# Seven smaller products for one more outer product of a feed-forward, and the order of the last loads

## The reference, cut to what matters

```python
D_FF = ((8 * D_MODEL // 3 + 255) // 256) * 256      # 2816 = 22 tiles of 128

def swiglu(h, w_gate, w_up, w_down):
    return (jax.nn.silu(h @ w_gate) * (h @ w_up)) @ w_down
```

## Time and profile before

| what | value |
|---|---|
| median of three runs | 5031.72 us (5031.61 to 5036.39) |
| the profiled execution | 5037.27 us, span 5035.5 us |
| TensorE matmul busy | 4921.3 us, 98% |
| VectorE busy | 3003.9 us, 60% |
| ScalarE busy | 865.2 us, 17% |
| feed-forward loop, block 1 to 10 | from 1384.24 us to about 1823.7 us |
| product with w_down | from 1829.79 us |

### The profile page before, as it was taken

The page is one execution under the profiler, slowest core; times in us unless marked ns, Lnnn a source line. Parts: engine busy times, 40 slices in busy tenths (PEclk is TensorE's granted clock), DMA queues, the critical chain, the costliest instruction groups (busy, mean ns, idle before and its releaser), DMA issues. The chain is left out here.

```text
span 5035.5 us, 68191 instructions
## 1 busy us (share of the span) xinstructions
PE 4921.3 (98%) x26175; PEld 3429.4 (68%) x26175; DVE 3003.9 (60%) x5245; ACT 865.2 (17%) x1673; POOL 72.0 (1%) x96
## 2 busy tenths in 40 slices
PE   8999999999999999999999799999999999999998
PEld 4545556855477754447666695959788696969695
DVE  3434445645388863553666575757667575767686
ACT  3611211133211100160444100000000000000010
POOL 0000000000000000000000000000000000000110
PEclk9999999999999999999999799999999999999999
DMA  5145032411222263433221354544445454545575
GB/s 209 40 148 182 26 105 96 152 59 62 61 67 71 72 204 100 159 109 117 106 90 57 114 185 147 194 164 160 167 158 189 150 181 177 185 172 201 180 284 217
DMA packets 396603, 694.44 MB, mean 138 GB/s; under 512 B 19896, under 2 KB 171003, under 8 KB 394234
## 3 DMA queue, kind: packets, MB, share of 16 engines
q1 hardware_dynamic: 382072, 641.80, 36.9%
q0 software_dynamic: 9920, 36.19, 2.0%
q10 hardware_dynamic: 4290, 12.11, 0.6%
HBM read 575.21 MB, written 114.83 MB: 137 GB/s over the span
## 5 line engine op out<-in xcount | busy, mean ns | idle before, releaser
L4880 PE MATMUL psum<-arena 128*128 128x128 f32 (+2 forms) x10752 | 1235.7, 276 | 2.9 <-issue 2.7
L4880 PEld LDWEIGHTS psum<-arena 128*128 128x128 f32 x10752 | 1225.7, 191 | 6.8 <-issue 6.8
L4859 PE MATMUL psum<-arena 128*128 128x512 f32 x1568 | 689.6, 595 | 2.8 <-DVE arena L4472 2.4
L4589 DVE TENSOR_TENSOR arena<-arena 128x1024 f32<-128x1024 f32 x448 | 539.4, 1224 | 64.5 <-issue 39.6
L4859 PEld LDWEIGHTS psum<-arena 128*128 128x128 f32 x1568 | 292.1, 190 | 363.3 <-issue 355.4
L1559 PE MATMUL psum<-arena 128*128 128x256 f32 x1400 | 305.4, 379 | 0.0
L1559 PEld LDWEIGHTS psum<-arena 128*128 128x128 f32 x1400 | 266.0, 190 | 44.7 <-issue 9.6
L1630 PE MATMUL psum<-arena 128*128 128x512 f32 x616 | 267.4, 596 | 5.9 <-DMA arena<-in_ffn_w_down 5.9
L4764 ACT ACTIVATE arena<-psum 128x288 f32<-128x288 f32 (+1 forms) x112 | 44.6, 398 | 1151.0 <-PE psum L4880 1072.6
L2219 PE MATMUL psum<-arena 128*128 128x256 f32 (+1 forms) x968 | 239.6, 407 | 1.4 <-PEq L112 1.4
L4467 DVE TENSOR_TENSOR arena<-arena 128x512 f32<-128x512 f32 x112 | 77.6, 693 | 252.5 <-PE psum L4865 157.7
(11 more groups left out here) (636 smaller groups left out, 6167.4 us busy)
## 6 DMA issues: line engine op xcount, KB each, us to landing
arena<-in_moe_w_gate SPq DMA_DIRECT2D x112, 1024.0 KB
arena<-in_moe_w_up SPq DMA_DIRECT2D x112, 1024.0 KB, 7.3
arena<-in_moe_w_down SPq DMA_DIRECT2D x112, 1024.0 KB, 6.7
y_dram<-zeros SPq DMA_DIRECT2D x1, 23040.0 KB
x_dram<-arena SPq DMA_DIRECT2D x32, 512.0 KB, 4.0
arena<-in_ab_w_in SPq DMA_DIRECT2D x7, 2048.0 KB, 8.9
arena<-z_dram SPq DMA_DIRECT2D x8, 1664.0 KB, 7.4
arena<-in_c_w_in SPq DMA_DIRECT2D x6, 2048.0 KB, 11.8
```

The source lines that it names most:

```text
L4589: V.tensor_tensor(to, left, right, ALU.subtract).then_inc(t_up, 1)
L4859: return nc.tensor.matmul(g.ps[:, bank, :], left, right, start=(i == 0), stop=(i == STEPS - 1))
L4880: last = nc.tensor.matmul(g.ps[:, bank, f * HT:f * HT + N // 2], right[:, k, f * P:(f + 1) * P], left[:, k, 0:N // 2], start=(k == 0), sto ...
```

## The change

Outer product 4 is made of seven smaller ones as well. So `SPLIT` gets a 4, a fourth set of inner token sums lies at column 33024 (until then free during the loop), and the VectorE order of a block changes: `inner_weights(n, 4)` comes ahead of `combine(n, 2)`, the difference t4 moves from between the combines of 2 and 3 to ahead of `combine(n, 4)`, and `combine(n, 4)` takes the place of the plain addition that made `part`. On ScalarE `take_corner(n, 4)` takes the place of `take_whole(n, 4)`. In SP's order of the loop, the load of raw quarter (1,1) is ahead of the store of Q22. At the end of the loop `bring_low(3)` is after product 4 instead of ahead of product 3, and the last piece of `low` is loaded in two halves, one after the last reader of raw quarter (1,0) and one after product 6, both ahead of the store of Q22. There are no new functions.

```diff
-    SPLIT = (2, 3, 5, 6, 7)
+    SPLIT = (2, 3, 4, 5, 6, 7)
@@ SP, loop
-                store(n, Q22, 1, 1)
                 sp.wait_ge(pm, groups_done(n, 6))
                 load(n + 1, 1, 1)
+                store(n, Q22, 1, 1)
@@ SP, after the loop
-            bring_low(3)
             sp.wait_ge(pm, groups_done(N, 3))
             bring_low(0)
             bring_low(1)
@@
             for t in (2, 3):
                 fetch_x(t, x_low)
+            bring_low(3)
             sp.wait_ge(pm, groups_done(N, 5))
             bring_low(2)
             load_low(1, 1, 2, b11)
+            sp.wait_ge(outer_made, 4 * N)
+            sp.dma_start(low[0][:, 0:2, :], quarter(1, 1)[:, 0:2, :]).then_inc(b11, 16)
+            sp.wait_ge(pm, groups_done(N, 6))
+            sp.dma_start(low[0][:, 2:4, :], quarter(1, 1)[:, 2:4, :]).then_inc(b11, 16)
             store(N, Q22, 1, 1)
-            sp.wait_ge(pm, groups_done(N, 6))
-            load_low(1, 1, 0, b11)
@@ TensorE
-                    whole_product(b, 4)
+                    pe.wait_ge(x_summed, 3)
+                    split_product(it, b, 4)
@@ ScalarE
                 take_corner(n, 3)
-                act.wait_ge(st_e, 16 * n)
-                take_whole(n, 4, e5)
+                take_corner(n, 4)
@@ VectorE, block_of_features
                 outer(n, t3, raw[1, 1], raw[0, 1])
+                inner_weights(n, 4)
                 dve.wait_ge(st_a, 16 * (2 * n - 1))
-                dve.wait_ge(whole, 2 * n + 1)
+                dve.wait_ge(whole, n + 1)
                 combine(n, 2, za, e1)
-                outer(n, t4, raw[1, 0], t2)
                 dve.wait_ge(st_b, 16 * n)
                 combine(n, 3, zb, e1, u)
                 gate(n, Q11)
                 inner_weights(n, 5)
-                dve.wait_ge(whole, 2 * n + 2)
-                V.tensor_tensor(part, u, e5, ALU.add).then_inc(joined, 1)
+                outer(n, t4, raw[1, 0], t2)
+                combine(n, 4, zb, u, part)
                 inner_weights(n, 6)
                 za_is_free(n)
                 combine(n, 5, za, u, u)
-                dve.drain()
-                V.tensor_tensor(e5, u, e5, ALU.add).then_inc(joined, 1)
+                dve.wait_ge(st_e, 16 * n)
+                dve.drain()
+                V.tensor_tensor(e5, u, zb[:, 0:4, :], ALU.add).then_inc(joined, 1)
@@ VectorE, ahead of the loop
-            for q in (2, 3, 6):
+            for q in (2, 3, 4, 6):
                 inner_tokens(q)
                 in_place(q).then_inc(x_summed, 1)
```

More of the change, by code:

```diff
@@ L1327, in ffn_stage @@
     RIGHTS = (raw[0, 0], raw[1, 0], t2, t1, t3, raw[1, 1], t4)
-    SPLIT = (2, 3, 5, 6, 7)
+    SPLIT = (2, 3, 4, 5, 6, 7)
     WAYS = len(SPLIT)
-    inner = [[A.at(o + 512 * q, 2, 256) for q in range(2)] + [A.at(last, 2, 256)] for o, last in ((24576, 25600), (26112, 27136), (30208, 31744), (35840, 36864), (37376, 38400))]
+    inner = [[A.at(o + 512 * q, 2, 256) for q in range(2)] + [A.at(last, 2, 256)] for o, last in ((24576, 25600), (26112, 27136), (33024, 34560), (30208, 31744), (35840, 36864), (37376, 38400))]
     ring = [[A.at(12288 + 1024 * r + 256 * q, 2, P) for q in range(4)] for r in range(2)]
@@ L1577, in _ @@
                     pe.wait_ge(hidden, 2)
-                    pe.wait_ge(combed, it * (2 * WAYS) + (WAYS * (c - 1) + 4))
+                    pe.wait_ge(combed, it * (2 * WAYS) + (WAYS * (c - 1) + 5))
                     whole_product(b, 1)
@@ L1583, in _ @@
                     pe.wait_ge(x_summed, 1)
-                    pe.wait_ge(combed, it * (2 * WAYS) + (WAYS * (c - 1) + 5))
+                    pe.wait_ge(combed, it * (2 * WAYS) + (WAYS * (c - 1) + 6))
                     split_product(it, b, 2)
@@ L1588, in _ @@
                     pe.wait_ge(outer_made, it * 8 + (4 * c - 2))
-                    pe.wait_ge(whole, it * 4 + (2 * c + 1))
+                    pe.wait_ge(whole, it * 2 + (c + 1))
                     split_product(it, b, 3)
@@ L1593, in _ @@
                     pe.wait_ge(combed, it * (2 * WAYS) + (WAYS * c + 1))
-                    whole_product(b, 4)
-                    pe.wait_ge(x_summed, 5)
+                    pe.wait_ge(x_summed, 3)
+                    split_product(it, b, 4)
+                    pe.wait_ge(x_summed, 6)
                     pe.wait_ge(outer_made, it * 8 + (4 * c - 1))
@@ L1601, in _ @@
                     pe.wait_ge(rb3, it * 64 + 32 * c)
-                    pe.wait_ge(x_summed, 3)
-                    pe.wait_ge(whole, it * 4 + (2 * c + 2))
+                    pe.wait_ge(x_summed, 4)
+                    pe.wait_ge(combed, it * (2 * WAYS) + (WAYS * c + 3))
                     split_product(it, b, 6)
-                    pe.wait_ge(x_summed, 4)
+                    pe.wait_ge(x_summed, 5)
                     pe.wait_ge(outer_made, it * 8 + 4 * c)
-                    pe.wait_ge(combed, it * (2 * WAYS) + (WAYS * c + 3))
+                    pe.wait_ge(combed, it * (2 * WAYS) + (WAYS * c + 4))
                     split_product(it, b, 7)
@@ L1613, in down @@
                 if n == 0:
-                    pe.wait_ge(b11, 48)
+                    pe.wait_ge(b11, 64)
                 elif m == 5 and t == 0:
@@ L1863, in take_from_high @@
                 dve.wait_ge(b21, 16)
-                dve.wait_ge(b11, 48)
+                dve.wait_ge(b11, 64)
                 V.tensor_tensor(high[:, k0:k1, :], high[:, k0:k1, :], low[q], ALU.subtract)
@@ L1888, in take_norm @@
                                 g.mix_g[:, 8:16].unsqueeze(2).broadcast_to([P, KD, P]), ALU.mult).then_inc(n_taken, 1)
-            credit(dve, whole, 2)
+            credit(dve, whole, 1)
             credit(dve, combed, WAYS)
```

## The result

The changed kernel took 5046.18 us (median of nine runs, 5039.73 to 5052.32), the kernel before 5035.94 us beside it. The ratio is 1.0021 with a 95% interval of 1.0013 to 1.0029, that is +6.5 to +14.6 us. I had forecast +6.0 us and 5037.7 us from a before of 5031.7; the direction holds, and so does what I said of the loop and of its end, but the size does not, and 5046.18 lies outside of my range of 5027 to 5044. Set against the before measured beside it, the forecast would have been 5041.9.

The account below looks back on a forecast made before the run. The prediction took VectorE to become the loop's bound, at 44.8 us a block, with transfers ending last at the joint. down(0) starting 6.0 us later, added to 5031.7, gave 5037.7 us; the range was 5027 to 5044.

Parts of the forecast that it names:

- What bounds the kernel: In the feed-forward loop: TensorE bounds the old 43.95 us block, with VectorE close behind at 4.3 us of slack.
- the wait that the new order makes: Before combine 3, VectorE waits for corner 3 behind the silu of Q11: 1.15 us lost per block.
- VectorE's ladder: VectorE's operations of one loop block laid out by starts: 43.61 us in the new order, above TensorE's 43.13.
- The waits named as slack: VectorE's waits in an old block for what ScalarE takes out of PSUM: 0.86, 1.09 and 2.35 us, 4.3 together.
- The block of 44.8: Length of a changed loop block: 43.61 plus 1.15 is 44.76, taken as 44.8, 0.85 us worse than 43.95.
- The joint: Loop end to down(0): the last half lands 30.3 us after first issue, 2.2 after the sums; down(0) 6.0 us later.
- Later parts: After down(0) starts: sums for down(1) have more room, stores and loads are issued 6 to 8 us later; nothing added.
- Case A: The forecast itself: VectorE bounds the loop at 44.8, transfers end last at the joint; 5037.7 us, 5033 to 5043, chance 0.50.
- B: Loop as in Case A, but transfers are in time at the joint; 5033 us, chance 0.14.
- C: The silu of Q11 doesn't hold corner 3 up, or an offset hides it; block 43.65, 5029 us, chance 0.14.
- D: TensorE stays the loop's bound, -8.15 us there; 5024 us, or 5021 with transfers in time, chance 0.08.
- E: More small gaps, or a clock falling within the loop; block 45.2 or more, +10 to +20 us, 5042 to 5052, chance 0.14.

Follow-up runs that it names:

- e1: The changed kernel with ScalarE taking corner 3 ahead of the silu of Q11; ratio to the kernel before 1.0007 (0.9998 to 1.0016).
- e4: The changed kernel with the difference t4 back between combine 2 and combine 3; ratio to the kernel before 1.0002 (0.9993 to 1.0011).
- e5: e1 with the fourth token sums elsewhere, so bring_low(3) is ahead of product 3 again and bring_low(1) waits for product 4; ratio to before 0.9993.
- e3: The kernel before with the SP part alone: last piece in halves and raw (1,1) load ahead of the store, bring_low(3) unmoved; ratio 0.9985 both times.
- e2: The changed kernel with the last w_down piece whole and, like the loop's raw (1,1) load, behind the store of Q22; ratio to before 1.0025.
- e7: The kernel before with 104 already met waits ahead of down(0), making TensorE's program 52 instructions longer; ratio 1.0009 (1.0000 to 1.0018).
- e8: e5 with t1 of the next block made between combine 7 and the gate of Q21; ratio to the kernel before 0.9993 (0.9984 to 1.0002).

## Why the prediction was off

**What bounds the kernel, and the wait that the new order makes: right.** VectorE's ladder became the bound, the wait before combine 3 was 1.07 us for a computed 1.15, and its removal in two ways (e1, e4) gave back 8.1 and 9.7 us of stage, 1.1 of the latter by the clock. The waits named as slack before combine 5 and before `part` went.

**The block of 44.8: too small by 0.2.** The four plain blocks have 44.85 to 44.90, but the others 45.21, because VectorE stops once for some 0.4 us between operations that wait for nothing. I had 0.36 us of such gaps in the comparison with the old block and took them to lie at waits that vanish. The eight blocks 2 to 9 took 360.3 us against 351.6 before, +8.7, where 8 x 0.85 = 6.8 was forecast; block 10 therefore began 8.4 us later and not 6.3, and `down(0)` came 7.8 us later, not 6.0.

**The joint: right in kind, nearly so in size.** The last half landed 30.1 us after the first issue, for a computed 30.3, and 1.9 us after the sums, for 2.2. That is 9.18 MB in about 28.4 us, 323 GB/s; the 341 GB/s that the Trainium skill has for a 1 MB transfer issued from GpSimd (DMA: Bandwidth & Descriptors, Bandwidth: Measured) isn't reached where 5.24 MB of it come in rows of one token tile. The clock took 1.4 us where I charged 2.26: TensorE stood 4.0 us and not 4.9, and the clock was down for 3.4 us where before it was down for 6.8. e5 shows that the backlog is the cause, e3 that without it the new order of the loads pays more, 6.6 us where it is 3.0 in the changed kernel (e2).

The two misses go against each other, +1.8 us by the blocks and -0.8 by the clock, and the stage costs 6.9 us for a forecast of 6.0.

**The time outside of the feed-forward, put at nothing: the step that failed.** The +6.0 us of the sum are the loop and the joint alone. Under "Later parts" I looked at what waits for transfers and sums, and added nothing; that TensorE's program gets longer, and that this can cost time in a stage whose instructions are the same, I didn't consider. The two stops in the experts have 2.0 to 2.9 us of idle time and cost 2.5 to 3.4 us, 3.1 on average. With this, the sums agree with the ratios to 0.0003 each, far inside the intervals: changed 6.9 + 3.1 = 10.0 us, 1.0020 (measured 1.0021 and 1.0019); e1 -1.2 + 3.1, 1.0004 (1.0007); e2 9.9 + 3.1, 1.0026 (1.0025); e3 -6.6, 0.9987 (0.9985); e4 -2.8 + 3.1, 1.0001 (1.0002); e5 -5.1 + 3.1, 0.9996 (0.9993); e7 0.6 + 3.1, 1.0007 (1.0009); e8 -8.3 + 3.1, 0.9990 (0.9993).

**The rest of the miss is the base.** The measured time is 8.5 us above the forecast: half is the change itself (10.2 us instead of 6.0), half the base. I took 5031.7, the middle of three runs; nine runs gave 5035.94. Runs of before lie between 5029.8 and 5041.1, so three are too few for a middle to 0.1%, and the range was placed 4 us too low. Case A's own upper end, 5043, would have been 5047 on that base.

**The rivals.** B (transfers in time) fell by the releaser, C (no wait at corner 3) by the 1.07 us, D (TensorE stays the bound) by the block. The Trainium skill (Perfetto Trace Analysis, Identifying the Most-Contended Engine) would have the engine with the highest occupancy improved first; by this D was to be expected. The page would not judge TensorE by its matmuls' busy time, 98%, but by its weight loads among others; by these too, 68% against VectorE's 60%, TensorE leads. The trace disagrees: TensorE's busy time did fall, from 4921.3 to 4915.8 us, while the kernel became slower. In the loop VectorE had no more than 4.3 us of slack in 43.95. E's size came true, +10.2 us, but in part by something else: of its two mechanisms, more small gaps made four of the eight blocks 45.2 us long (45.04 on average), while the clock never fell within the loop.

## What to carry to other kernels

Before a product is split to relieve the busiest engine, lay out one period of the next engine operation by operation: 4.3 us of slack against 4.3 us of added work left no room for a 1.1 us round trip through ScalarE. Two consecutive operations that both depend on a third engine need its order of instructions looked at; either work between them or the other order there makes the wait free. A transfer that is issued earlier gains only the time in which the queue would have run empty, so what else stands in that queue decides: the same new order of the last loads gave 6.6 us alone and 3.0 us behind `bring_low(3)`. And where a change is worth 0.2%, the base needs more than three runs.

## What the runs showed of the hardware that I had not expected

- A TensorE program longer by 52 of 39809 instructions, 2.4 ms ahead, gives two stops of 0.9 to 1.6 us each in a later stage whose instructions are the same; together they delay all that follows by 2.5 to 3.4 us. The profiles with the program at its old length never show them (four), those with the longer program always do (eight).
- After equal stops of 2.22 us the granted clock fell in one run (1826.1 us, e5_corner_first_tile3_early) and not in another (e8_t1_in_the_silu_wait); after 1.56 us it fell in neither of two. Shorter stops can do it as well, and by this unchanged stages scatter: in all twelve profiles TensorE stops for 1.6 to 1.9 us near 2425 us, for a transfer of `ht_dram` (1.66 us before 2429.26 in the changed kernel, 1.70 us before 2426.72 in the first profile of before). The clock then fell for 3.4 us in nine of them, at 2429.98 in the changed kernel, and in three not, the first profile of before among them; the two ways differ by 1.7 us.
- VectorE, with nothing to wait for, stops for some 0.4 us four times in the changed kernel's blocks 2 to 9, at the same four operations in both profiles. The kernel before has such stops too (0.43 us in block 1, 0.44 us in block 7), and its blocks stay at 43.95 us: there the slack of 4.3 us takes them up. What the stops are is open.
